# A fifth gate panel inside the attention passes, and one PSUM bank for the later attention outputs

## The chip, the cores and the metric

The kernel runs on one core of a Trainium2 chip. The metric is the device time of one execution in microseconds. Before the change it is 1691.17 us, the median of three runs that span 1689.38 to 1691.74 us.

## What is computed

Four transformer-like layers run on one sequence of 256 tokens with 1024 channels, all in float32. The first two layers (the "first block") are the ones touched here. Cut to what matters, each of them is

```
h = rms_norm(x, attn_pre_gain);  u = h @ w_in            # q, k, v of two attentions, g_nsa, g_a, g_b
o_a = swa_sink_attention(qa, ka, va, sinks)               # windowed softmax attention with sinks
o_b = g0 * o_compressed + g1 * o_selected + g2 * o_window # gates = sigmoid(g_nsa)
mixed = sigmoid(g_a) * (o_a @ w_branch_a) + sigmoid(g_b) * (o_b @ w_branch_b)
x = x + rms_norm(mixed @ w_out, attn_post_gain)
x = x + rms_norm(conv_ffn(rms_norm(x, ffn_pre_gain), ...), ffn_post_gain)
```

g_a and g_b are 2048 of the columns of `h @ w_in`. The last two layers (the "second block") are feed-forward parts and another attention; the change does not touch them.

## The kernel before, in words

**Precision and tiles.** Every large product is made from split operands: a float32 value is a high part that TensorE takes exactly plus the rest. Activations stand as high and low parts side by side (hsA, hsB: 256 + 256 columns of tokens). A weight chunk of 1 MB lands in one of three raw buffers (`RAW`), ScalarE copies it to the high part (L616), VectorE subtracts to get the low part (L1001, `split_to`), and both stand in one of four slots (`RING`). A *wide* tile takes two matmuls for each of its k steps: the high weights against 512 columns (L1582) and the low weights against 256 (L1587); ScalarE then copies the second half of the bank to `low` (`low_copy`) and VectorE adds the two (`tile_sum`, L1009). A *narrow* tile (`NARROW`) adds three matmuls of 256 columns in place (L1580, L1581, L1586) and needs only one copy by ScalarE (`whole_copy`). Tiles have fixed PSUM banks (`tile_bank`: tile number modulo 4, unless in `EXTRA` or `PLACED`).

**The gate panels.** g_a and g_b are made in eight panels of two tiles each (one tile for a, one for b). The first four (`EARLY`) are narrow tiles, made before and in the first passes of the attention. The other four are wide tiles in the *branch* stage behind the attention, in the order of the list `BRANCH`: products with w_branch ("mix", four tiles of four k steps) alternate with gate panels ("gate", two tiles of eight k steps). Panel j's results go to `gate_place(j)`; ScalarE applies the sigmoid, and GpSimd (POOL) multiplies and adds (L1501 to L1505) into MX; ScalarE and VectorE split that into MS, which the following product with w_out reads (L1698 to L1700). VectorE overwrites TA and SG buffers only once POOL is through with them (`mix_ready`).

**The attention passes.** `MAPS` lists 18 score maps: six of the first attention, then for each of six units one compressed-plus-selected map (br 1) and one window map (br 2). The loop over i is written out on every engine as a software pipeline: in pass i TensorE makes the scores of map i (L1850, L1853), transposes the probabilities of map i - 4 (L1873) and makes the value products of map i - 5 (L1900, L1904). VectorE masks and takes maxima (L1254), ScalarE exponentiates (L619), VectorE inverts the sums (L1280), POOL scales (L1493), ScalarE copies the transposed probabilities out of PSUM (PT, L616). The value products accumulate into output number o: 0 to 5 for the first attention, 6 to 11 for the second, where the products of br 1 open and those of br 2 close the accumulation. Output o sits in bank 2 + o % 2. It leaves PSUM in two steps, a ScalarE copy to hsB (L616) and a VectorE subtraction (L1266, counts `o_done`); TensorE waits for the output before the last one that used the bank. Gate panel 3 is made in passes 1 and 3 (`early_tile`), and the first two tiles of mix 0 in passes 21 and 22.

**Queues.** SP issues all weight loads in chunk order; a load waits until VectorE has split the chunk three places earlier. In the attention the splits reach two chunks past panel 3, that is mix 0 and gate panel 4; the split of the next chunk (mix 1) stands at the end of the passes.

## Time and profile before

| quantity | value |
|---|---|
| median of 3 runs | 1691.17 us (1689.38 to 1691.74) |
| profiled execution, first to last instruction (span) | 1688.0 us |
| PE busy / weight loads busy | 1672.5 us (99%) / 1443.9 us (86%) |
| DVE / ACT / POOL busy | 1215.7 / 1034.5 / 698.7 us |
| DMA, mean rate | 182 GB/s |
| chain that ended last | PE 92%, DVE 3%, ACT 2%, DMA 2% |
| granted TensorE clock | 1.000 over the span |

The profile gives the profiled execution's span; no time of its own around the span is shown for it. The span is 3.2 us under the median of the runs (1.4 to 3.7 us under the three of them), which is the start and end that the span leaves out. Matmuls are pipelined and their ends are modelled, so the start of one row to the start of the next is the reading to trust, not the duration in the row. First-block layer 1 has its attention passes from about 84 to 132 us and its branch stage to about 171 us; layer 2 repeats them some 367 us later.

### The profile page before, as it was taken

What the parts mean: (1) busy time and instruction counts of PE and PEld (TensorE: products, weight loads), DVE (VectorE), ACT (ScalarE), POOL (GpSimd) and SP (SyncE); (2) the same over time, 40 slices, a digit from 0 to 9 for tenths busy, and PEclk for the clock granted to TensorE, in tenths of its full rate; (3) what the DMA queues carried; (4) which work ended last, traced back from release to release, by engine and by line L of the source; (5) the groups of instructions that cost most, each with busy time, mean ns of one, the idle gap of its engine ahead of it and who ended that gap; (6) DMA issues with size and microseconds to landing.
All of it is one profiled execution on the core that took longest, in us unless ns stands there. A gap on an engine that the chain in (4) does not pass through costs nothing.

```text
span 1688.0 us, 26353 instructions
## 1 busy us (share of the span) xinstructions
PE 1672.5 (99%) x9878; PEld 1443.9 (86%) x9878; DVE 1215.7 (72%) x1810; ACT 1034.5 (61%) x1901; POOL 698.7 (41%) x662
## 2 busy tenths in 40 slices
PE   8999999999999999999999999999999999999998
PEld 7968888889968988888888979888898889788887
DVE  7877799958868899867664757666576647576663
ACT  6787766656786766565554657554655536575543
POOL 4154176601255276407750052663076600527630
PEclk9999999999999999999999999999999999999999
DMA  8925586565816666649666626866496565358662
GB/s 242 245 69 175 144 231 178 178 218 164 238 27 200 180 195 174 233 128 256 184 199 200 225 75 181 219 173 226 126 250 190 185 224 201 99 150 215 184 212 75
DMA packets 416354, 306.67 MB, mean 182 GB/s; under 512 B 10179, under 2 KB 369013, under 8 KB 416226
## 3 DMA queue, kind: packets, MB, share of 16 engines
q1 hardware_dynamic: 415536, 304.44, 61.6%
q8 instruction: 79, 1.29, 0.3%
q0 software_dynamic: 688, 0.53, 0.1%
q14 instruction: 49, 0.40, 0.1%
q10 hardware_dynamic: 2, 0.00, 0.0%
HBM read 303.89 MB, written 1.05 MB: 181 GB/s over the span
## 4 chain that ended last, share of the span: by engine, by line
PE 92%; DVE 3%; ACT 2%; DMA 2%; issue 1%; SPq 0%; DVEq 0%; ACTq 0%
PE bank L1582 31%; PE bank L1587 15%; PE bank L1698 9%; PE bank L1700 9%; PE bank L1699 9%; PE bank L1661 3%; PE bank L1658 3%; PE bank L1650 3%; DMA raw<-in_w_in 1%; PE bank L1580 1%; DVE whl L1001 1%; PE bank L1581 1%; PE bank L1586 1%; PE bank L1631 1%; PE bank L1904 1%; PE bank L1873 1%
## 5 line engine op out<-in xcount | busy, mean ns | idle before, releaser
L1001 DVE TENSOR_TENSOR whl<-raw,whl 128x1024 fp32r<-128x1024 f32 (+2 forms) x572 | 741.4, 1319 | 174.1 <-ACT whl L616 169.5
L616 ACT ACTIVATE whl<-raw 128x1024 fp32r<-128x1024 f32 (+2 forms) x572 | 581.5, 1040 | 162.1 <-PE bank L1700 102.0
L1582 PE MATMUL bank<-hsA,whl 128*128 128x512 f32 x2112 | 668.5, 396 | 0.0
L1587 PEld LDWEIGHTS bank<-hsA,whl 128*128 128x128 f32 x2112 | 396.8, 188 | 92.5
L1587 PE MATMUL bank<-hsA,whl 128*128 128x256 f32 x2112 | 415.2, 278 | 0.0
L1582 PEld LDWEIGHTS bank<-hsA,whl 128*128 128x128 f32 x2112 | 324.3, 189 | 2.6 <-issue 2.2
L616 ACT ACTIVATE low<-bank 128x256 f32<-128x256 f32 (+1 forms) x356 | 133.4, 379 | 256.3 <-PE bank L1582 237.0
L1442 POOL TENSOR_TENSOR HB<-CB,UB 128x256 f32<-128x256 f32 x88 | 123.7, 1406 | 337.8 <-ACT CB L619 337.2
L1698 PE MATMUL bank<-whl,hid 128*128 128x512 f32 x528 | 205.9, 390 | 0.0
L1700 PE MATMUL bank<-whl,hid 128*128 128x512 f32 x528 | 205.4, 389 | 0.0
L1699 PE MATMUL bank<-whl,hid 128*128 128x512 f32 x528 | 205.4, 389 | 0.0
L1009 DVE TENSOR_TENSOR UB<-bank,low 128x256 f32<-128x256 f32 x264 | 109.0, 417 | 111.2 <-ACT low L616 111.1
L1443 POOL TENSOR_TENSOR hid<-CB,UB 128x256 fp32r<-128x256 f32 x88 | 145.0, 1648 | 0.0
L1442 POOL TENSOR_TENSOR HB<-CB 128x256 f32<-128x256 f32 x44 | 63.1, 1434 | 139.0 <-ACT CB L619 139.0
L1700 PEld LDWEIGHTS bank<-whl,hid 128*128 128x128 f32 x528 | 99.1, 188 | 20.7
L1699 PEld LDWEIGHTS bank<-whl,hid 128*128 128x128 f32 x528 | 99.1, 188 | 20.4
L1698 PEld LDWEIGHTS bank<-whl,hid 128*128 128x128 f32 x528 | 99.1, 188 | 20.1
L1338 DVE SCALAR_TENSOR_TENSOR CB<-UB,convT,CB 128x256 f32<-128x256 f32 x176 | 114.0, 706 | 0.0
L1444 POOL TENSOR_TENSOR hid<-HB,hid 128x256 fp32r<-128x256 f32 x132 | 109.6, 830 | 10.3
L1661 PE MATMUL bank<-hsA,whl 128*128 128x256 f32 x448 | 92.6, 284 | 0.3 <-DVE whl L1001 0.3
L1658 PE MATMUL bank<-hsA,whl 128*128 128x256 f32 x448 | 90.5, 283 | 0.0
L1520 POOL MEMSET CU<- 128x4 f32 x2 | 0.2, 103 | 191.0 <-DVE U L1009 191.0
(234 smaller groups left out, 2355.5 us busy)
## 6 DMA issues: line engine op xcount, KB each, us to landing
raw<-in_ffn_w_up SPq DMA_DIRECT2D x176, 512.0 KB, 5.3
raw<-in_ffn_w_down SPq DMA_DIRECT2D x120, 512.0 KB, 4.5
raw<-in_w_in SPq DMA_DIRECT2D x96, 512.0 KB, 6.5
raw<-in_ffn_w_gate SPq DMA_DIRECT2D x88, 512.0 KB, 4.0
raw<-in_w_out SPq DMA_DIRECT2D x32, 512.0 KB, 4.6
raw<-in_ffn_w_down SPq DMA_DIRECT2D x24, 256.0 KB, 3.0
G<-in_norm_g SPq DMA_DIRECT2D x12, 512.0 KB, 7.5
raw<-in_cmp_w SPq DMA_DIRECT2D x8, 512.0 KB, 6.4
```

Source lines behind the costliest of these rows:

```text
L616: return nc.scalar.activation(out_, in_, func, **kw)
L1001: v.tensor_tensor(lo, w_, hi, ALU.subtract).then_inc(wlo_ready, 1)
L1338: ins = v.scalar_tensor_tensor(y[:, n, :], UB[:, j % 2, n, k:S + k], convT[:, k, at:at + 1], y[:, n, :], ALU.mult, ALU.add)
L1442: g_.tensor_tensor(HB[:, j % 2, :], x, y, ALU.mult)
L1443: seq.link(g_.tensor_tensor(dst[:, 0:S], x, y, ALU.mult))
L1582: return mm(out_[:, 0:2 * n], whi[slot][:, at:at + P], rhs[:, 0:2 * n], start=x == 0, stop=False, **g32)
L1587: return mm(out_[:, n:2 * n], wlo[slot][:, at:at + P], rhs[:, 0:n], start=False, stop=False, **g32)
L1658: return mm(out_, whi[c % RING][:, at(m, k):at(m, k) + P], both(k, 1), start=False, stop=j == 0 and k == KD - 1, **g32)
L1661: return mm(tile_bank(t + m)[:, S:2 * S], wlo[c % RING][:, at(m, k):at(m, k) + P], hsA[:, k, 0:S], start=False, stop=j > 0 and k == KD - 1 ...
L1698: mm(y, hi, whi[s][:, x * HALF:x * HALF + HALF], start=k == k_first, stop=False, **g32)
L1699: mm(y, lo, whi[s][:, x * HALF:x * HALF + HALF], start=False, stop=False, **g32)
L1700: ins = mm(y, hi, wlo[s][:, x * HALF:x * HALF + HALF], start=False, stop=k == k_end, **g32)
```

## The change

`EARLY` becomes 5. Gate panel 4 becomes two narrow tiles in bank 3, each cut into four quarters of two k steps (six matmuls of 256 columns). Quarters are made in passes 12 to 15 (first tile) and 17 to 20 (second tile), between the transposes and the value products. Since bank 3 holds the tiles, outputs 6 to 11 all use bank 2, and TensorE waits before opening output o (o > 6) for the output just before it. ScalarE copies the finished tiles in passes 16 and 21 into a new buffer SG4. Panel 4's chunk comes ahead of mix 0's; one more chunk (gate panel 5) is split in passes 18 to 20. The branch stage keeps three gate panels, with panel 7 between mix 2 and mix 3 in place of panels 6 and 7.

```diff
@@ -79,8 +79,8 @@
 
 
 
-EARLY = 4
-BRANCH = [("mix", 0), ("gate", 4), ("mix", 1), ("gate", 5), ("mix", 2), ("gate", 6), ("gate", 7), ("mix", 3)]
+EARLY = 5
+BRANCH = [("mix", 0), ("gate", 5), ("mix", 1), ("gate", 6), ("mix", 2), ("gate", 7), ("mix", 3)]
 SKEW = 4
 RINGP = 5
 
@@ -243,6 +243,7 @@
     st = sb("st", [P, RINGP, 4, 4])[0]
     stc = sb("stc", [P, 4, 16])[0]
     KC = sb("KC", [P, 2, 2 * N_CMP])[0]
+    SG4 = sb("SG4", [P, 2, S])[0]
     VC = sb("VC", [P, 8, HD], at=cq_at)[0]
 
 
@@ -407,6 +408,7 @@
     EXTRA = {t + m: 4 + m for t in EXTRA for m in range(2)}
 
     PLACED = {p["early"][3][1] + m: 2 + m for p in PLAN.one for m in range(2)}
+    PLACED.update({p["early"][4][1] + m: 3 for p in PLAN.one for m in range(2)})
     PLACED.update({p["fill"] + m: 4 + m for p in PLAN.one for m in range(2)})
 
     NARROW = {t + m for L, p in enumerate(PLAN.one) for _, t in p["in"][3 if L else 1:6] + p["early"] for m in range(2)} | \
@@ -428,13 +430,19 @@
 
         if j == 3:
             return tm[:, :, :]
+        if j == 4:
+            return SG4[:, :, :]
         return SGE[:, 2 * j:2 * j + 2, :] if j < EARLY else SG[:, 2 * (j % 2):2 * (j % 2) + 2, :]
+
+    def o_bank(o):
+
+        return bank[2 + o % 2 if o < 6 else 2]
 
     def o_places(o):
 
         g, qb, hs = UNITS[o % 6]
         j0, nj = 4 * (o // 6) + hs[0] // 2, len(hs) // 2
-        src = bank[2 + o % 2][:, 0:nj * P].rearrange("d (j q) -> d j q", q=P)
+        src = o_bank(o)[:, 0:nj * P].rearrange("d (j q) -> d j q", q=P)
         return (lambda part: hsB[:, j0:j0 + nj, part * S + qb * P:part * S + qb * P + P]), src
 
     def score_place(i, x, keys):
@@ -791,7 +799,7 @@
                         f(HCV[:, :, 0:N_CMP].rearrange("p (g r) c -> p g r c", g=2),
                           x.rearrange("p (g c) -> p g c", g=2).unsqueeze(2).broadcast_to([P, 2, 4, N_CMP]),
                           ACT.Gelu_apprx_tanh, bias=b1).then_inc(cmp_hid, 1)
-            third, fourth = p["early"][2][1], p["early"][3][1]
+            third, fourth, fifth = [p["early"][j][1] for j in (2, 3, 4)]
             whole_copy(third, gate_place(2)[:, 0, :])
             act.preload_act_table_set("natural_log_exp_and_others")
             whole_copy(third + 1, gate_place(2)[:, 1, :])
@@ -813,10 +821,12 @@
                     act.wait_ge(pv_done, done + m + 1)
                     dst, src = o_places(o)
                     f(dst(0), src, ACT.Copy).then_inc(o_hi, 1)
+                if i in (16, 21):
+                    whole_copy(fifth + i // 21, gate_place(4)[:, i // 21, :])
                 m = i - SKEW
                 if m == len(MAPS) + 1:
                     low_copy(p["fill"] + 1)
-                    split_to(p["early"][3][0] + 3)
+                    split_to(p["early"][4][0] + 3)
                 if 0 <= m < len(MAPS):
                     act.wait_ge(pt_ready, done + m + 1)
                     if m >= 2:
@@ -846,8 +856,10 @@
                 if i == 2:
                     act.wait_ge(cmp_x, L + 1)
                     f(PC[:, :, :, 0:N_CMP], PC[:, :, :, 0:N_CMP], ACT.Exp, scale=SCALE).then_inc(cmp_e, 1)
+                if i in (18, 19):
+                    split_to(p["early"][4][0] + 2, i - 18)
                 if m == len(MAPS) - 1:
-                    split_to(p["early"][3][0] + 3, 0)
+                    split_to(p["early"][4][0] + 3, 0)
 
 
             def sigmoids(j):
@@ -858,7 +870,7 @@
                 if 0 < j < 3:
                     low_copy(p["fill"] + 1 + j)
                 if j == 0:
-                    act.wait_ge(tile_out, fourth + 2)
+                    act.wait_ge(tile_out, fifth + 2)
                 sigmoids(j)
 
             def mixed_hi(x):
@@ -880,7 +892,7 @@
                 if kind == "gate":
                     act.wait_ge(tile_out, t + 2)
                     sigmoids(x)
-                if kind == "gate" and x == 6:
+                if kind == "gate" and x == 7:
                     mixed_hi(2)
             mixed_hi(3)
             nxt = token_major(n0 + 1, p["up"][0][1])
@@ -1280,6 +1292,8 @@
                     v.reciprocal(s_[:, 3, 0:nh], s_[:, 1, 0:nh]).then_inc(inv_ready, 1)
                 if i < 2:
                     split_to(p["early"][3][0] + 2, i)
+                if i in (19, 20):
+                    split_to(p["early"][4][0] + 2, i - 19)
                 if i == 2:
                     cmp_scores()
                 if i == 4:
@@ -1315,7 +1329,7 @@
                             split_to(c + 3 if x else c + 2)
                     if x == 0:
                         split_to(c + 3)
-                if kind == "gate" and x == 6:
+                if kind == "gate" and x == 7:
                     mixed_lo(2)
             mixed_lo(3)
             nxt = token_major(n0 + 1)
@@ -1765,6 +1779,22 @@
                 c, t = p["early"][j]
                 chunk_here(c)
                 tile(t + m, c, [(in_pair(m, k), hsA[:, k, :]) for k in range(KD)], beside)
+
+            def gate_quarter(m, quarter):
+
+                c, t = p["early"][4]
+                out_ = tile_bank(t + m)[:, 0:S]
+                if quarter == 0:
+                    chunk_here(c)
+                    pe.wait_ge(o_done, 12 * L + 6)
+                    pe.wait_ge(tile_out, t + m)
+                for k in range(2 * quarter, 2 * quarter + 2):
+                    hi, lo = [w_[c % RING][:, in_pair(m, k):in_pair(m, k) + P] for w_ in (whi, wlo)]
+                    mm(out_, hi, hsA[:, k, 0:S], start=k == 0, stop=False, **g32)
+                    mm(out_, hi, hsA[:, k, S:2 * S], start=False, stop=False, **g32)
+                    ins = mm(out_, lo, hsA[:, k, 0:S], start=False, stop=k == KD - 1, **g32)
+                if quarter == 3:
+                    ins.then_inc(sum_ready, 1)
 
             first = 3 if THREE[n0] else 1
             for c in range(10):
@@ -1879,6 +1909,8 @@
                     for qb in range(2):
                         ins = nc.tensor.transpose(bank[1][:, S + qb * P:S + qb * P + P], PC[:, qb, :, :].rearrange("p h c -> p (h c)"), ident)
                     ins.then_inc(cmp_t, 1)
+                if 12 <= i < 21 and i != 16:
+                    gate_quarter(i // 17, i - (17 if i > 16 else 12))
                 m = i - SKEW - 1
                 if 0 <= m < len(MAPS):
                     u, br = MAPS[m]
@@ -1890,18 +1922,18 @@
                     if m < 2:
                         pe.wait_ge(tile_out, fourth + 2)
                     if br < 2 and o >= 2:
-                        pe.wait_ge(o_done, 12 * L + o - 1)
+                        pe.wait_ge(o_done, 12 * L + (o if o > 6 else o - 1))
 
                     def every_other(ap, e):
                         return ap.rearrange("k (j e q) -> k j e q", e=2, q=P)[:, :, e, :]
                     if br == 1:
                         for x, h in enumerate(hs):
                             j, r = x // 2 * P, HD * (x % 2)
-                            mm(bank[2 + o % 2][r:r + HD, j:j + P], VC[:, h, :], PCT[:, qb * P:qb * P + P],
+                            mm(o_bank(o)[r:r + HD, j:j + P], VC[:, h, :], PCT[:, qb * P:qb * P + P],
                                start=j == 0, stop=False, **g32)
                     for kb in range(qb + 1):
                         for e in range(2):
-                            ins = mm(bank[2 + o % 2][HD * e:HD * e + HD, 0:n // 2], V1[:, br, kb, HD * g:HD * g + HD],
+                            ins = mm(o_bank(o)[HD * e:HD * e + HD, 0:n // 2], V1[:, br, kb, HD * g:HD * g + HD],
                                      every_other(PT[:, m % 2, kb * n:kb * n + n], e),
                                      start=br == 0 and kb == 0, stop=br != 1 and kb == qb, **g32)
                     ins.then_inc(pv_done, 1)
```

## Rows read from the trace of the kernel before

**Rows 1.** The page's part 1: busy time of each engine.

```profile
PE 1672.5 (99%) x9878; PEld 1443.9 (86%) x9878; DVE 1215.7 (72%) x1810; ACT 1034.5 (61%) x1901; POOL 698.7 (41%) x662
```

**Rows 2.** Waits of PE, whole span (us in total, times, longest).

```profile
PE bank L1904 <- ACT PT L616: 1.9, 6, 0.4
```

**Rows 3.** Stretches (us, engines busy, PEclk, DMA share, GB/s): passes 12 on; branch stage.

```profile
109.50:125.80 16.30, 16.30 (x151) 10.31 (x149) 10.40 (x56) 14.78 (x46) 10.53 (x21) 1.00 0.01 2
...
132.20:150.00 17.80, 17.80 (x104) 15.49 (x103) 14.84 (x19) 14.42 (x31) 10.66 (x10) 1.00 0.71 184
```

**Rows 4.** Timeline of PE, passes 13 to 21 in extract (start, us, instruction); layer 2.

```profile
112.38 0.44 PE L1900 MATMUL bank<-U,VC 128*64 128x128 f32 x4
...
116.82 0.69 PE L1853 MATMUL bank<-KSW,QR 64*128 64x512 f32 x1
...
117.88 0.66 PE L1873 MATMUL bank<-const,PB 128*128 128x128 f32 x4
118.47 0.66 PE L1904 MATMUL bank<-PT,V 128*64 128x128 f32 x8
119.06 0.66 PE L1873 MATMUL bank<-const,PB 128*128 128x128 f32 x4
...
124.99 0.44 PE L1900 MATMUL bank<-U,VC 128*64 128x128 f32 x4
...
480.63 0.69 PE L1853 MATMUL bank<-KSW,QR 64*128 64x512 f32 x1
...
484.26 0.69 PE L1853 MATMUL bank<-KSW,QR 64*128 64x512 f32 x1
```

**Rows 5.** Timeline of PE: branch stage, first tile of gate panel 4 and first of mix 1.

```profile
132.28 0.39 PE L1582 MATMUL bank<-hsA,whl 128*128 128x512 f32 x1
...
137.85 0.39 PE L1582 MATMUL bank<-hsB,whl 128*128 128x512 f32 x1
```

**Rows 6.** Timeline of PE: a whole narrow tile in pass 1, first and last rows.

```profile
84.68 0.38 PE L1580 MATMUL bank<-hsA,whl 128*128 128x256 f32 x1
84.90 0.28 PE L1581 MATMUL bank<-hsA,whl 128*128 128x256 f32 x1
...
87.53 0.28 PE L1581 MATMUL bank<-hsA,whl 128*128 128x256 f32 x1
87.73 0.48 PE L1850 MATMUL bank<-U 64*128 64x256 f32 x1
```

**Rows 7.** Timeline of PE: two 256-column matmuls between transposes, entry of the feed-forward part.

```profile
199.58 0.66 PE L1631 MATMUL bank<-const,H 128*128 128x128 f32 x4
199.99 0.48 PE L1650 MATMUL bank<-hsA,whl 128*128 128x256 f32 x2
200.31 0.60 PE L1631 MATMUL bank<-const,H 128*128 128x128 f32 x4
```

**Rows 8.** Timeline of DVE: subtractions of outputs 6, 8 and 10.

```profile
113.38 0.42 DVE L1266 TENSOR_TENSOR hsB<-bank,hsB 128x256 fp32r<-128x256 f32 x1 [0.54 <-ACT hsB L616]
...
120.34 0.29 DVE L1266 TENSOR_TENSOR hsB<-bank,hsB 128x128 fp32r<-128x128 f32 x1 [0.45 <-ACT hsB L616]
...
124.82 0.29 DVE L1266 TENSOR_TENSOR hsB<-bank,hsB 128x128 fp32r<-128x128 f32 x1 [1.83 <-ACT hsB L616]
```

**Rows 9.** Timeline of POOL: sum of panel 5; first rows of panels 6 and 7.

```profile
161.28 1.63 POOL L1505 TENSOR_TENSOR MX<-TA 128x256 f32<-128x256 f32 x1
169.72 0.75 POOL L1501 TENSOR_TENSOR TA<-TA,SG 128x256 f32<-128x256 f32 x1 [6.80 <-DVE TA L1009]
...
174.07 0.74 POOL L1501 TENSOR_TENSOR TA<-TA,SG 128x256 f32<-128x256 f32 x1 [0.24 <-DVE TA L1009]
```

**Rows 10.** Timeline of DVE: low part of panel 7's mixture.

```profile
176.99 0.42 DVE L1296 TENSOR_TENSOR MS<-MX,MS 128x256 fp32r<-128x256 f32 x1 [1.90 <-ACT MS L616]
```

**Rows 11.** Timeline of PE: first and ninth matmul of the product with w_out.

```profile
171.29 0.39 PE L1698 MATMUL bank<-whl,MS 128*128 128x512 f32 x1
...
173.11 0.39 PE L1700 MATMUL bank<-whl,MS 128*128 128x512 f32 x1
```

## The prediction, made before the change was run

> **What bounds the kernel now.** I read the page's busy times first. They say PE 99% [rows 1], but a busy PE row is a pipelined row, so that alone proves nothing. The waits of PE come next: in the attention it waited for the copy of transposed probabilities, 1.9 us in six waits over both layers [rows 2], and the timeline has those in passes 5 to 9, ahead of the first quarter. Then the stretches: from pass 12 to pass 20 PE has no idle time, while ACT is busy 14.8 of 16.3 us and DVE 10.4; in the branch stage PE has none either [rows 3]. What decides is the distance from one start to the next in PE's timeline. Transposes start at 117.88, value products at 118.47, the next transposes at 119.06 [rows 4]: 0.59 us each, again and again, and layer 2 keeps the same step of 3.63 us for two passes [rows 4]. Other engines' waits would make such distances uneven. So PE's own stream sets the time from pass 10 of the attention to the end of the branch stage, with ACT close behind.
>
> The consequence for this change: quarters placed in passes 12 to 20 find no holes. They push the passes apart by what they cost, and the time comes back in the branch stage as one gate panel less. The forecast is a difference of two nearly equal terms.
>
> **Part 1, what leaves the branch stage.** Gate panel 4 begins at 132.28 and the next chunk at 137.85 [rows 5]: 5.57 us of PE in each layer, with nothing else limiting it. Wide or narrow makes no difference in columns: 8 x (512 + 256) against 8 x 3 x 256.
>
> **Part 2, what the quarters cost.** Inside a narrow tile 22 matmuls pass between 84.90 and 87.53, 0.12 us each, so six of them are 0.72. The whole tile takes 87.73 - 84.68 = 3.05 us where 24 x 0.12 = 2.88, so going from attention products into it and out again costs 0.17 [rows 6]. If every quarter pays that on top of what was there, it costs 0.89: the upper bound. But the 0.59 us from four transposes to the value products is partly the start-up of a waited group. Where no wait follows, four transposes take 199.99 - 199.58 = 0.41, and two matmuls of 256 columns behind them, with a waited group after, 0.32 [rows 7]. Six would take 0.32 + 4 x 0.12 = 0.80, so from transposes to value products through a quarter would be 1.21 instead of 0.59: 0.62 more. That is the lower bound, and the nearest row for a quarter without waits of its own. The first quarter of each tile has waits (for the chunk, for bank 3, for the tile before), so I give it the 0.89. Per layer: 6 x 0.62 + 2 x 0.89 = 5.5 us, between 8 x 0.62 = 5.0 and 8 x 0.89 = 7.1. Parts 1 and 2 together: -0.07 us per layer, between -0.6 and +1.55.
>
> **Part 3, one bank for outputs 6 to 11.** Now TensorE may open output o only when the one before has been copied by ACT and subtracted by DVE. Both stand in queues: ACT's copy behind the exponentials of the pass before, DVE's subtraction behind the maxima. There are five such hand-overs per layer, in passes 13, 15, 17, 19 and 21. Pass 13: the subtraction of output 6 ended at 113.38 + 0.42 = 113.80, and the value products would start at 112.38 + 0.89 + 0.62 = 113.89 with two quarters ahead [rows 4, 8]: no stall. Pass 17, with no quarter in pass 16 to lend time: products wanted at 119.06 + 0.59 + 0.89 = 120.54 in the old frame, subtraction over at 120.34 + 0.29 = 120.63 [rows 4, 8], some 0.2 late with the signal. Pass 21 has no quarter: wanted at 124.99, subtraction over at 124.82 + 0.29 = 125.11 [rows 4, 8], again 0.2. Passes 15 and 19 have slack: a quarter each, and no exponentials any more in passes 18 and 19. So 0.4 us per layer. Below: 0, if ACT, which gets more room as passes grow, is earlier. Above: each hand-over as late as output 6's in the old frame, 113.80 - 112.38 = 1.4 behind the wanted time, less the 0.62 of a quarter: 0.8 at four places and 1.4 at pass 21, 4.6 us per layer.
>
> The Trainium skill, in "Perfetto Trace Analysis", section "Matmuls", says that independent matmul groups should rotate through PSUM banks so that the emptying of one lies beside the next. It speaks against this part. By the rule every hand-over would be exposed, and the sum would be near the upper end just given; by the rows the quarter itself lies beside the emptying. No row of before has all outputs in one bank.
>
> **Part 4, the shorter branch stage.** Taking a panel from between mix 2 and mix 3 leaves POOL, DVE and ACT less time for the last mixtures. In the old frame mix 2's matmuls end at 132.28 + 4 x 5.57 = 154.56, the sum of panel 5 on POOL at 161.28 + 1.63 = 162.91 [rows 5, 9]. DVE may write panel 7's sums only then, into the buffer of panel 5. PE needs the first of those sums at mix 3's third tile, 154.56 + 1.5 x 5.57 = 162.9: a stall of up to 0.5, or none, since POOL's 1.63 lies beside a DVE split that now comes later. From there to the last low part: DVE's sums, a half split, low parts, sums of mix 3, an estimated 3.4 us of DVE work; panel 6 on POOL, 174.07 - 169.72 less 0.24 of waiting = 4.1 [rows 9]; a signal, 0.2; panel 7 to the end of its low part, 176.99 + 0.42 - 174.07 = 3.3 [rows 9, 10]. Together 11.0, so 173.1 to 173.9. PE reads that part after 33 matmuls of the product with w_out, (173.11 - 171.29) / 8 = 0.2275 us each, so at 171.29 + 7.5 - 5.57 = 173.2 [rows 11]; before, it wanted it at 178.8 and had it at 177.4. The old slack of 1.4 us is gone. I take 0.3 us per layer, between 0 and 1.3.
>
> **Edits costed at nothing.** The chunk split moved into passes 18 to 20 (two ScalarE copies, two VectorE subtractions) falls where both have idle time: no exponentials after pass 17, and DVE sat idle 1.83 us before output 10's subtraction [rows 8]. SP loads one chunk earlier, into a stretch with a DMA share of 0.01 [rows 3]. The two narrow copies replace two `low` copies on ACT, and two sums of DVE go. The fifth sigmoid pair moves ahead of panel 5's copies. If ACT's cover were gone, these would feed the hand-overs of part 3.
>
> **The sum.** Per layer -0.07 + 0.4 + 0.3 = +0.63, for two layers +1.3 us. The profiled span goes from 1688.0 to 1689.3. The runs' median stands 3.2 us above the span, so 1692.5 us. A measurement of this kernel can tell about 0.2% (3.4 us) from no change; this forecast is no difference to be seen. Its own range, with parts 2 to 4 within half of their bounds, is 1689.5 to 1694.5. Chance 0.66.
>
> **Rivals.**
>
> *The passes have hidden holes (faster).* Weight loads are busy 10.3 of 16.3 us in the later passes against 15.5 of 17.8 in the branch stage [rows 3]. If the difference were room, eight quarters would cost nothing: -2 x 5.57 + 1.4 for parts 3 and 4 = -9.7, 1681.4 us. For it: that share, and passes that are as long as ACT's work. Against: the even starts [rows 4]; short matmuls (64 x 512, 128 x 128) need few weight loads for their time. Chance 0.08. The skill's "Perfetto Trace Analysis", section "Identifying the Most-Contended Engine", calls matmul busy time a poor measure and wants the share of weight loads instead; by that reading the attention has headroom and this rival is the forecast. The distances between starts agree with the first half of the rule and not with the second.
>
> *A quarter saves nothing (slower).* Each costs 0.89 us [rows 6]: +1.55 per layer, with parts 3 and 4 +2.25, for both +4.5, 1695.7 us. For it: the only whole narrow tile inside attention passes shows that price. It decides from about 0.82 us per quarter on. Chance 0.16.
>
> *The single bank is late at every hand-over (slower).* The place is TensorE's wait for `o_done` before products of br 1 in passes 13 to 21; the price is 4.6 us per layer, so 2 x (-0.07 + 4.6 + 0.3) = +9.7, 1700.9 us. It decides once the subtraction ends more than 1.2 us (transposes and quarter) after the closing products. For it: ACT is busy 91% of that stretch [rows 3], and its copy queues behind exponentials. Against: slower passes give ACT room, and half the hand-overs were costed with none needed. Chance 0.10, mostly in a milder form near 1697.
>
> **How the numbers follow.** Likeliest case: 1692.5. Faster by over 0.2%: the first rival, 0.08. Slower by over 0.2%: 0.16 + 0.10 = 0.26. Within: 0.66. The range is 1688.5 (lower bounds of all parts, -1.2 us, with the runs' own scatter) to 1698.0, which takes in the second rival and the mild form of the third; outside stay the first rival and the far end of the third.
>
> **What would show it.** Right: two value-product starts around a quarter 1.2 us apart; passes 12 to 20 longer by 5 to 6 us per layer; branch stage shorter by 5.6; new waits of PE L1900 on DVE L1266 of a few tenths, in passes 17 and 21; at most a few tenths at L1698 or L1700 on MS. Wrong: passes no longer than before (first rival), quarters 0.9 us apart in price (second), waits on L1266 above 1 us (third), or PE waits at the end of the branch stage of over 1 us, which would be part 4 mis-sized.

## The result and the profile after

| | kernel before | changed kernel |
|---|---|---|
| median of 11 runs each | 1690.89 us | 1694.30 us |
| lowest to highest | 1688.76 to 1691.74 | 1693.18 to 1695.51 |
| profiled execution (span) | 1691.17 (1688.0) | 1694.68 (1692.9) |
| ratio, 95% interval | | 1.0023 [1.0015, 1.0031] |

The change costs 3.4 us by the medians (3.9 by the ratio). The prediction said 1692.5 with a range of 1688.5 to 1698.0, which holds the result. The likeliest case was "no difference to be seen", below 0.2%, with a chance of 0.66; the result lies just above that bound, in the case that had 0.26. It is on the side that the sum of +1.3 us pointed to, but at two to three times its size. So most of what follows asks where the other two microseconds come from.

The page's first part, after, answers [rows 1]:

```profile
PE 1675.2 (99%) x9910; PEld 1447.0 (85%) x9910; DVE 1213.2 (72%) x1806; ACT 1032.7 (61%) x1901; POOL 694.5 (41%) x662
```

PE has 32 more matmuls: wide tiles of 512 and 256 columns have become narrow ones of three times 256, with equal columns. The page's sums tell nothing more. The waits of PE over the whole span (us in total, times, longest) say where to look:

```profile
PE bank L1936 <- ACT PT L624: 2.0, 6, 0.4
PE bank L1932 <- DVE hsB L1278: 1.1, 4, 0.4
...
PE bank L1596 <- DVE SG L1021: 0.3, 2, 0.2
```

The first answers [rows 2] and is unchanged. The other two are new: L1932 is the first value product of a hand-over of the single bank, L1596 a tile of the branch stage.

**The layer in pieces.** Between the transposes of pass 12 and the transposes behind the product with w_out, nothing comes in from outside the change, so I take the distance between their starts as the measure S of every kernel below. PE's timeline before, at both ends:

```profile
110.63 0.66 PE L1873 MATMUL bank<-const,PB 128*128 128x128 f32 x4
...
191.70 1.03 PE L1631 MATMUL bank<-const,H 128*128 128x128 f32 x8
```

Before, S was 191.70 - 110.63 = 81.07 us, in layer 2 the same to 0.01. PE's timeline after (start, us, instruction):

```profile
111.45 0.66 PE L1903 MATMUL bank<-const,PB 128*128 128x128 f32 x4
111.86 0.36 PE L1793 MATMUL bank<-hsA,whl 128*128 128x256 f32 x1
...
112.75 0.65 PE L1936 MATMUL bank<-PT,V 128*64 128x256 f32 x4
113.33 0.66 PE L1903 MATMUL bank<-const,PB 128*128 128x128 f32 x4
...
114.78 0.44 PE L1932 MATMUL bank<-U,VC 128*64 128x128 f32 x4
...
122.28 0.66 PE L1936 MATMUL bank<-PT,V 128*64 128x128 f32 x8
122.87 0.66 PE L1903 MATMUL bank<-const,PB 128*128 128x128 f32 x4
124.60 0.66 PE L1932 MATMUL bank<-U,VC 128*64 128x128 f32 x8 [0.36 <-DVE hsB L1278]
...
131.49 0.66 PE L1903 MATMUL bank<-const,PB 128*128 128x128 f32 x4
132.35 0.44 PE L1932 MATMUL bank<-U,VC 128*64 128x128 f32 x4 [0.21 <-DVE hsB L1278]
...
139.64 0.39 PE L1596 MATMUL bank<-hsA,whl 128*128 128x512 f32 x1
...
145.21 0.39 PE L1596 MATMUL bank<-hsB,whl 128*128 128x512 f32 x1
...
148.32 0.47 PE L1596 MATMUL bank<-hsB,whl 128*128 128x512 f32 x1 [0.16 <-DVE SG L1021]
...
151.26 0.47 PE L1596 MATMUL bank<-hsA,whl 128*128 128x512 f32 x1
...
156.92 0.39 PE L1596 MATMUL bank<-hsB,whl 128*128 128x512 f32 x1
...
173.65 0.39 PE L1712 MATMUL bank<-whl,MS 128*128 128x512 f32 x1
...
194.35 1.04 PE L1645 MATMUL bank<-const,H 128*128 128x128 f32 x8
```

S is now 194.35 - 111.45 = 82.90 us: +1.83 per layer, and layer 2 gives the same +1.83. To read it: the distance from a pass's four transposes to its value products was 0.59 us in all of passes 12 to 21 [rows 4]. In pass 12 it is now 112.75 - 111.45 = 1.30. Passes 14, 15, 18 and 20 also show 1.30 and pass 19 shows 1.29, so a quarter costs 0.71, in layer 2 too (within 0.01). Pass 16, which has none, still shows 0.59. Three passes show more: 13 has 1.45, which is 0.15 above 1.30; 17 has 124.60 - 122.87 = 1.73, 0.43 above; 21, which has no quarter, has 0.86, 0.27 above 0.59.

| per layer, us | forecast | measured |
|---|---|---|
| panel 4 leaves the branch stage | -5.57 | -5.57 |
| eight quarters | +5.5 | 8 x 0.71 = +5.68 |
| hand-overs of the bank | +0.4 (0, 0.2, 0.2) | +0.85 (0.15, 0.43, 0.27 in passes 13, 17, 21) |
| mix 1 and gate panel 6 | 0 | +0.57 |
| product with w_out | +0.3 | +0.29 |
| sum | +0.63 | +1.82 |

The fourth line was not forecast. Mix 1 begins at 145.21 and panel 6 at 151.26, which is 6.05 us instead of 5.57; panel 6 takes 156.92 - 151.26 = 5.66, 0.09 more than 5.57. For the last line, 194.35 - 173.65 = 20.70 stands against 20.41 before.

Two layers give +3.66 of the 4.9 us between the spans. A further 0.84 us arises at the start, ahead of anything changed. The transposes of HE early in the attention start at 80.75 after (L1775) and at 79.91 before (L1761). None of the nine experiments touches this part, and in their profiles the same instruction starts anywhere from 79.35 to 81.91, so I put the 0.84 down to scatter of that size; its cause is not shown. About 0.4 us lies in the last feed-forward part and was not followed up. It does not recur between the medians, whose difference of 3.4 is accounted for by 3.66.

### The profile page after: what moved, and what is told of

It reads as the page before. It is cut to its first block, busy times and chain, and to the rows that moved or that the text cites. A ratio compares the mean times of both kernels' runs of the same rounds, so it can differ in the third digit from the quotient of the medians.

```text
span 1692.9 us, 26417 instructions
## 1 busy us (share of the span) xinstructions
PE 1675.2 (99%) x9910; PEld 1447.0 (85%) x9910; DVE 1213.2 (72%) x1806; ACT 1032.7 (61%) x1901; POOL 694.5 (41%) x662
## 3 DMA queue, kind: packets, MB, share of 16 engines
q8 instruction: 79, 1.29, 0.3%
## 4 chain that ended last, share of the span: by engine, by line
PE 88%; ACT 4%; DVE 3%; DMA 2%; issue 1%; POOL 1%; SPq 1%; DVEq 0%; ACTq 0%; POOLq 0%
PE bank L1596 30%; PE bank L1601 15%; PE bank L1712 9%; PE bank L1714 8%; PE bank L1713 8%; PE bank L1675 3%; PE bank L1672 3%; PE bank L1664 2%; DMA raw<-in_w_in 2%; DVE whl L1013 1%; ACT whl L624 1%; PE bank L1594 1%; PE bank L1645 1%; PE bank L1936 1%; PE bank L1595 1%
## 5 line engine op out<-in xcount | busy, mean ns | idle before, releaser
L1596 PE MATMUL bank<-hsA,whl 128*128 128x512 f32 x2080 | 658.5, 396 | 0.0
L1601 PEld LDWEIGHTS bank<-hsA,whl 128*128 128x128 f32 x2080 | 390.8, 188 | 91.0
L1601 PE MATMUL bank<-hsA,whl 128*128 128x256 f32 x2080 | 408.9, 278 | 0.0
L1596 PEld LDWEIGHTS bank<-hsA,whl 128*128 128x128 f32 x2080 | 319.4, 189 | 2.9 <-issue 2.6
L624 ACT ACTIVATE low<-bank 128x256 f32<-128x256 f32 x352 | 131.4, 379 | 258.6 <-PE bank L1596 239.2
L1712 PE MATMUL bank<-whl,hid 128*128 128x512 f32 x528 | 205.9, 390 | 0.0
L1714 PE MATMUL bank<-whl,hid 128*128 128x512 f32 x528 | 205.5, 389 | 0.0
L1714 PEld LDWEIGHTS bank<-whl,hid 128*128 128x128 f32 x528 | 99.1, 188 | 20.6
L1712 PEld LDWEIGHTS bank<-whl,hid 128*128 128x128 f32 x528 | 99.1, 188 | 20.1
L1675 PE MATMUL bank<-hsA,whl 128*128 128x256 f32 x448 | 92.6, 284 | 0.0
L1672 PE MATMUL bank<-hsA,whl 128*128 128x256 f32 x448 | 90.5, 283 | 0.0
```

The source lines that it names most:

```text
L624: return nc.scalar.activation(out_, in_, func, **kw)
L1596: return mm(out_[:, 0:2 * n], whi[slot][:, at:at + P], rhs[:, 0:2 * n], start=x == 0, stop=False, **g32)
L1601: return mm(out_[:, n:2 * n], wlo[slot][:, at:at + P], rhs[:, 0:n], start=False, stop=False, **g32)
L1672: return mm(out_, whi[c % RING][:, at(m, k):at(m, k) + P], both(k, 1), start=False, stop=j == 0 and k == KD - 1, **g32)
L1675: return mm(tile_bank(t + m)[:, S:2 * S], wlo[c % RING][:, at(m, k):at(m, k) + P], hsA[:, k, 0:S], start=False, stop=j > 0 and k == KD - 1 ...
L1712: mm(y, hi, whi[s][:, x * HALF:x * HALF + HALF], start=k == k_first, stop=False, **g32)
```

## The experiments

S of each kernel (layer 1; layer 2 agrees within 0.05), against 81.07 before and 82.90 of the changed kernel, with the run time and, where there are several runs, the ratio to the kernel before:

| kernel | S | per layer | median | ratio |
|---|---|---|---|---|
| bank only | 85.80 | +4.7 | 1700.21 | 1.0052 [1.0037, 1.0068] |
| sigmoids of panel 4 later | 82.16 | +1.1 | 1693.53 | 1.0014 [1.0005, 1.0023] |
| quarters in odd passes | 82.87 | +1.8 | 1694.61 | 1.0025 [1.0015, 1.0034] |
| three edits together | 81.99 | +0.92 | 1692.97 | 1.0006 [0.9997, 1.0015] |
| half splits one pass later | 81.77 | +0.70 | 1692.57 | 1.0007 [0.9998, 1.0016] |
| one half split on ACT | 81.34 | +0.28 | 1690.94 | 1.0003 [0.9993, 1.0012] |
| whole tiles | 85.47 | +4.4 | 1699.62, one run | |
| quarters behind the value products | 85.76 | +4.7 | 1701.32, one run | |
| own place for panel 7 | 82.58 | +1.5 | 1694.80, one run | |

The kernel before was timed again beside them: 1691.19 us beside the first four rows, 1690.32 beside "one half split on ACT", 1691.24 beside the rest. So a median is to be held against its own partner. The last three ratios include 1: what separates those kernels from each other is S, which repeats to 0.05 us, and not the run time.

### The single bank alone

The kernel before, with the new bank rule and nothing else:

```diff
+    def o_bank(o):
+        return bank[2 + o % 2 if o < 6 else 2]
...
-                        pe.wait_ge(o_done, 12 * L + o - 1)
+                        pe.wait_ge(o_done, 12 * L + (o if o > 6 else o - 1))
```

> The kernel before with one edit: outputs 6 to 11 use bank 2 and TensorE waits for the output just before. No quarters, four early panels. Theory A (a quarter lies beside the emptying of the bank and hides most of it; alone, the single bank is dear): in the kernel before, the value products of passes 13, 15 and 17 start at 112.38, 116.01 and 119.64, and the subtractions they would now wait for end at 113.80, 117.39 and 120.63, so they come 1.0 to 1.5 us late; with stalls that give ACT room in between, 2.5 to 4.5 us per layer over the five hand-overs, 1696 to 1700 us in all. Rival B (the hand-over costs little whatever lies beside it, and what the changed kernel lost comes from the cut of the tile): under 0.5 us per layer, 1691 to 1692 us. The branch stage keeps its length, 4 chunks of 5.57 us from gate panel 4 on, in both.

S is 85.80: 4.7 us per layer, above what was expected. PE's waits and its timeline in passes 13 and 17:

```profile
PE bank L1904 <- ACT PT L620: 5.3, 4, 1.5
PE bank L1904 <- DVE hsB L1270: 3.5, 6, 1.1
```

```profile
113.02 0.66 PE L1877 MATMUL bank<-const,PB 128*128 128x128 f32 x4
...
115.17 0.44 PE L1904 MATMUL bank<-U,VC 128*64 128x128 f32 x4 [1.49 <-ACT PT L620]
...
123.05 0.66 PE L1877 MATMUL bank<-const,PB 128*128 128x128 f32 x4
...
124.78 0.66 PE L1904 MATMUL bank<-U,VC 128*64 128x128 f32 x8 [1.07 <-DVE hsB L1270]
```

From transposes to value products it takes 2.15, 1.80, 1.73, 1.10 and 0.86 us in passes 13, 15, 17, 19 and 21, where 0.59 was enough: 1.56 + 1.21 + 1.14 + 0.51 + 0.27 = 4.69. This is the whole of the 4.7. All five hand-overs are late, not only two.

The profile names ACT's copy to PT for the waits of passes 13 and 15. By the code that is not what these products wait for: the copy to PT that pass 13 needs is the one of pass 12, and it was over by 113.14. They wait for the subtraction of output 6, which ends at 115.02, and the product starts 0.15 later at 115.17; the profile names the instruction that ended last, here the copy for the next pass, 0.03 later. All of these are waits for the bank.

 With the quarters in, the five cost 0.15, 0, 0.43, 0 and 0.27. So the quarters hide 3.8 of 4.7 us. In pass 17 the sum is exact: 1.14 - 0.71 = 0.43. In pass 21, which has no quarter, the 0.27 is the same in both kernels.

The Trainium skill ("Perfetto Trace Analysis", section "Matmuls") says that independent groups should rotate through PSUM banks. Alone, the single bank costs what the rule warns of, and this run agrees with it; the changed kernel keeps to one bank and pays 0.85, since other matmuls fill the time in which the bank is emptied.

### The sigmoids of panel 4 behind mix 0

```diff
-                sigmoids(j)
+                if j < 4:
+                    sigmoids(j)
...
+                    if n_ == 1:
+                        sigmoids(4)
```

The second place is in ACT's loop over `BRANCH`, behind the copies of gate panel 5 and the chunk splits around them.

> The changed kernel with the fifth panel's two sigmoids moved on ACT from before gate panel 5's chunk splits to behind them. In the trace of the changed kernel the third tile of mix 1 starts 0.33 us late behind the sum of panel 5, mix 1 takes 6.05 us in place of 5.57 and the gate panel after it 5.66. Theory A (these 0.61 us of sigmoids on ACT delay the split, the split delays VectorE's sums of panel 5, and these hold TensorE): mix 1 back to 5.57 to 5.65, the next panel to 5.57, 0.5 to 0.6 us per layer, 1693.1 to 1693.4 us in all against 1694.3. Rival B (VectorE and POOL contend for SBUF there, whatever ACT does): mix 1 stays at 6.0, 1694.3 us.

S falls by 0.74, to 82.16. PE's timeline shows mix 1 at its old length:

```profile
145.49 0.39 PE L1599 MATMUL bank<-hsB,whl 128*128 128x512 f32 x1
...
151.06 0.39 PE L1599 MATMUL bank<-hsA,whl 128*128 128x512 f32 x1
```

151.06 - 145.49 = 5.57; panel 6 takes 5.58. Together that is the 0.57. A further 0.17 is gained in the product with w_out (20.53 instead of 20.70 in layer 1; in layer 2 it is 20.59, a gain of 0.12). This settles the unforecast line. The chain in the changed kernel is one of queues. ACT, then DVE:

```profile
142.71 0.72 ACT L627 ACTIVATE SG<-SG 128x256 f32<-128x256 f32 x2
143.32 2.00 ACT L624 ACTIVATE whl<-raw 128x1024 fp32r<-128x1024 f32 x2
```

```profile
144.41 3.43 DVE L1013 TENSOR_TENSOR whl<-raw,whl 128x1024 fp32r<-128x1024 f32 x2 [2.37 <-ACT whl L624]
147.77 0.74 DVE L1021 TENSOR_TENSOR SG<-bank,low 128x256 f32<-128x256 f32 x2
```

The fifth sigmoid pair takes 143.32 - 142.71 = 0.61 us on ACT, ahead of the high parts of a chunk. DVE waits for these (2.37 idle), subtracts for 3.4 us, and only then forms the sums of gate panel 5, which free the two banks that mix 1 needs for its third tile. That tile would have started at 145.21 + 5.57 / 2 = 147.99 and started at 148.32. DVE's busy share of 72% hides this. What counts is that the bank of a matmul stands behind a 3.4 us job in a queue whose start is set by another queue.

### Quarters in the odd passes

The hand-overs fall in odd passes. So two quarters each went into passes 13, 15 and 17, one each into 19 and 21:

```diff
-                if 12 <= i < 21 and i != 16:
-                    gate_quarter(i // 17, i - (17 if i > 16 else 12))
+                for tile_, quarter_ in {13: [(0, 0), (0, 1)], 15: [(0, 2), (0, 3)], 17: [(1, 0), (1, 1)], 19: [(1, 2)], 21: [(1, 3)]}.get(i, []):
+                    gate_quarter(tile_, quarter_)
```

The second tile's copy moves from pass 21 to 22 with it.

> The changed kernel with the same eight quarters in other passes: two in pass 13, two in 15, two in 17, one in 19, one in 21, none in 12, 14, 18 and 20; the second copy moves from pass 22 of ACT in place of 21. All hand-overs of bank 2 that TensorE waits for then have one or two quarters in front. In the changed kernel passes 13, 17 and 21 lose 0.15, 0.43 and 0.27 us to the hand-over, 0.85 per layer. Theory A (the hand-overs make that loss): the idle time in front of L1932 goes to 0 to 0.2 us in all, each quarter still costs 0.70 to 0.73 us, 0.7 to 0.85 us per layer gained, about 1692.7 us. Rival B (the loss belongs to the number of switches between transposes, quarter and value products): eight switches become five, which would save 3 x 0.17 = 0.5 us per layer in the cost of the quarters, with the idle time left as it is. Rival C (two quarters in one pass delay the transposed probabilities for ACT and the next scores): other waits of 0.3 us and more appear in passes 14, 16 and 18, nothing gained.

S stays (82.87): nothing is gained. Rival C expected that, but not in this way: passes 14, 16 and 18 keep their 0.59 and show no new wait. Passes 15 and 17 show 2.02 = 0.59 + 2 x 0.71 + 0.01, and pass 21 shows 1.30, so the waits of 17 and 21 are gone; pass 13 keeps its 0.14. But pass 19 has 1.94 for one quarter:

```profile
127.02 0.65 PE L1903 MATMUL bank<-const,PB 128*128 128x128 f32 x4
...
128.96 0.44 PE L1932 MATMUL bank<-U,VC 128*64 128x128 f32 x4 [0.58 <-ACT PT L624]
```

The time removed at two places (0.43 + 0.27) came back at a third (0.64). The profile names ACT's copy to PT again, but again that is the copy for the next pass; the one that pass 19 needs, in the first row below, was long over. ACT's timeline, then DVE's:

```profile
126.54 0.60 ACT L624 ACTIVATE PT<-bank 128x512 f32<-128x512 f32 x1 [1.01 <-PE bank L1903]
127.03 1.05 ACT L624 ACTIVATE whl<-raw 128x1024 fp32r<-128x1024 f32 x1
127.98 0.37 ACT L624 ACTIVATE hsB<-bank 128x256 fp32r<-128x256 f32 x1
```

```profile
128.39 0.42 DVE L1278 TENSOR_TENSOR hsB<-bank,hsB 128x256 fp32r<-128x256 f32 x1 [2.31 <-ACT hsB L624]
```

The half split that the change moved into pass 18 holds ACT for 1 us. The copy of output 9 stands behind it, and the subtraction behind that. The subtraction ends at 128.81, and the product starts 0.15 later, at 128.96: this is still a wait for the bank. From the transposes of pass 18 to that start the chain takes 128.96 - 125.85 = 3.11 us. PE needs 0.59 + 0.58 + 1.30 = 2.47 for the same way with one quarter in it, so it waits 0.64. In the changed kernel two quarters lie on the way, one of them in pass 18, and PE needs 128.79 - 125.62 = 3.17, just longer than the chain; there the same split cost nothing.

### Three edits together

Quarters in the odd passes, the later sigmoids, and a place of its own for gate panel 7:

```diff
+        if j == 7:
+            return SGE[:, 0:2, :]
...
-                    if x >= EARLY + 2:
-                        dve.wait_ge(mix_ready, 8 * L + x - 1)
```

> The two edits above together, and panel 7 written to the place of panel 0 in place of that of panel 5, so that VectorE's sums of panel 7 don't wait for POOL. Theory A: what is left of the change is 8 x 0.71 - 5.57 = +0.11 us per layer; 1691.2 us, no difference to the kernel before (1690.9), with the passes 5.7 us longer per layer and the branch stage 5.6 us shorter. The late start of the last k step of the product with w_out (0.29 us per layer) goes too, because the sums of panel 7 come some 2 us earlier. Rival B (something of the change costs apart from the three waits, 1.8 us per layer in all): 1692.5 us or more stay.

S is 81.99, +0.92 per layer, where the remaining wait of pass 19 (0.64) and that of pass 13 (0.14) with 0.11 from the quarters make 0.89. All chunks of the branch stage take 5.57 and the product with w_out 20.41, as before the change. So the branch terms are gone, as expected; that nearly the whole gain should come was not met, since the attention's term is moved rather than removed. The median of 1692.97 lies where Rival B had it, but what stays is again waits for the bank, not another cost of the change.

### The half splits one pass later

ACT's half splits go from passes 18 and 19 to 19 and 20, DVE's from 19 and 20 to 20 and 21, all else as in the three edits:

```diff
-                if i in (18, 19):
-                    split_to(p["early"][4][0] + 2, i - 18)
+                if i in (19, 20):
+                    split_to(p["early"][4][0] + 2, i - 19)
```

> three_fixes with the two halves of the chunk split moved by one pass: on ACT from passes 18 and 19 to 19 and 20, on DVE from 19 and 20 to 20 and 21. In three_fixes the value products of pass 19 came 1.94 us behind their transposes where 1.30 is the price of a quarter, with 0.58 us idle behind ACT's copy of the transposed probabilities. Theory A (the ACT half split of 1.05 us in pass 18, which has no quarter there, holds that copy up): pass 19 takes 1.30 to 1.40, pass 20 at most 0.2 more than before; the stretch from the transposes of pass 12 to those behind the product with w_out goes from 81.99 to 81.4 to 81.6 us in both layers (81.07 in the kernel before), about 1692.0 us where three_fixes had 1692.97. Rival B (ACT's copies of outputs hold it up): pass 19 stays at 1.94.

S is 81.77, a little more than expected. Pass 19 is back at 1.30, so the half split was the cause; what it had held up there was the copy of output 9, not the copy to PT that Theory A names. But pass 21 shows 1.70. ACT in pass 20, and PE's waits for a bank over both layers:

```profile
131.27 1.05 ACT L626 ACTIVATE whl<-raw 128x1024 fp32r<-128x1024 f32 x1
132.22 0.27 ACT L626 ACTIVATE hsB<-bank 128x128 fp32r<-128x128 f32 x1
```

```profile
PE bank L1935 <- DVE hsB L1283: 0.7, 2, 0.3
```

The second half now stands ahead of the copy of output 10. The same microsecond of ACT reappears as a wait in whichever hand-over follows it, unless a quarter covers it.

### One half split on ACT in the passes

So only the first half stays in a pass (19); the second falls to the split that ACT does anyway at the end of the attention. DVE takes its halves in passes 20 and 22.

```diff
-                if i in (18, 19):
-                    split_to(p["early"][4][0] + 2, i - 18)
+                if i == 19:
+                    split_to(p["early"][4][0] + 2, 0)
```

> later_splits with the second ACT half of the chunk split moved from pass 20 to behind the last copy of transposed probabilities in pass 21, and VectorE's from 21 to 22. In later_splits pass 21 took 1.70 us from transposes to value products where a quarter makes it 1.30, because ACT's copy of output 10 stood behind that half split (131.27 to 132.3). Theory A (every loss of the change is a place in ACT's queue, and all are now named): pass 21 at 1.30, the stretch from the transposes of pass 12 to those behind the product with w_out 81.35 us in both layers, that is 0.28 us above the kernel before: 0.11 for 8 quarters at 0.71 against one wide panel at 5.57, and 0.14 in pass 13. In all about 1691.8 us, no difference. Rival B (the split has to be paid somewhere in the passes or at their end, since ACT has no idle time left): pass 21 at 1.30 but the same 0.4 us appears in pass 22 or at the first tiles behind the passes, stretch 81.7.

PE's timeline in pass 21:

```profile
129.76 0.66 PE L1906 MATMUL bank<-const,PB 128*128 128x128 f32 x4
...
131.06 0.44 PE L1935 MATMUL bank<-U,VC 128*64 128x128 f32 x4
```

There is no wait, 131.06 - 129.76 = 1.30, and pass 19 has the same distance. S is 81.34, +0.28 per layer: 0.11 by which eight quarters cost more than the panel they replace, and 0.15 in pass 13. The ratio is 1.0003 [0.9993, 1.0012]. It is the best version that I ran, and it does not beat the kernel before: with all waits but the one of pass 13 gone, the change is worth nothing. Whether that last 0.15 can be removed was not tried; without it the change would still cost 0.1 us per layer.

### Whole tiles instead of quarters

Is it the cutting into quarters that costs? All four quarters of a tile in one pass, 12 and 17:

```diff
+                for tile_, quarter_ in {12: [(0, 0), (0, 1), (0, 2), (0, 3)], 17: [(1, 0), (1, 1), (1, 2), (1, 3)]}.get(i, []):
+                    gate_quarter(tile_, quarter_)
```

> The changed kernel with the same matmuls uncut: all four quarters of the first tile in pass 12, of the second in pass 17. Theory A (a quarter costs its six matmuls and nothing for the cut, since the start-up of the waited group behind it is hidden): transposes to value products 0.59 + 4 x 0.72 = 3.45 us, in both passes, the same sum as 8 quarters at 0.71; but the hand-overs without a quarter grow, 0.3 to 0.5 in pass 13, about 1.2 in pass 15, 0.5 in 19, 0.27 in 21, so the stretch from the transposes of pass 12 to those behind the product with w_out comes to 84 to 84.5 us (82.90 in the changed kernel). Rival B (every cut costs 0.17 us, so six fewer cuts save 1.0 us per layer, and hand-overs depend little on where the quarters are): 82.0 us.

PE's timeline in passes 12 and 13:

```profile
111.19 0.66 PE L1903 MATMUL bank<-const,PB 128*128 128x128 f32 x4
...
114.64 0.65 PE L1936 MATMUL bank<-PT,V 128*64 128x256 f32 x4
115.23 0.66 PE L1903 MATMUL bank<-const,PB 128*128 128x128 f32 x4
...
116.33 0.44 PE L1932 MATMUL bank<-U,VC 128*64 128x128 f32 x4 [0.45 <-DVE hsB L1278]
```

114.64 - 111.19 = 3.45, or 2.86 for 24 matmuls: 0.715 per six, the same as a quarter. The cuts cost nothing. What is lost is cover: passes 13, 15, 19 and 21 exceed the 0.59 us by 0.51, 1.21, 1.36 and 0.28, and S ends at +4.4, 1 us above the expectation, in which the stall of pass 19 was taken at 0.5.

### Quarters behind the value products

The same quarters, placed after each pass's value products instead of between transposes and value products (the block moves behind the increment of `pv_done`).

> The changed kernel with each quarter made behind the value products of its pass in place of ahead of them. Theory A (only the order on TensorE between closing and opening an output counts, and a quarter lies between them either way): passes 12 to 21 take the same time within 0.4 us per layer, stretch 82.5 to 83.3 us (82.90). Rival B (the place between transposes and value products is worth its cover of ACT's copy of the transposed probabilities): transposes to value products grow past 0.59 us in several passes, 1 us per layer and more is lost. Rival C (behind the value products a quarter pays both switches, 0.17 us): 8 x 0.17 = 1.4 us per layer, 84.3.

PE's timeline, passes 12 and 13:

```profile
112.92 0.65 PE L1934 MATMUL bank<-PT,V 128*64 128x256 f32 x4
113.51 0.39 PE L1793 MATMUL bank<-hsA,whl 128*128 128x256 f32 x1
...
114.33 0.60 PE L1903 MATMUL bank<-const,PB 128*128 128x128 f32 x4
...
115.67 0.44 PE L1930 MATMUL bank<-U,VC 128*64 128x128 f32 x4 [0.74 <-ACT PT L624]
```

From value products to the next transposes it takes 114.33 - 112.92 = 1.41, where 0.58 was enough, so here a quarter costs 0.83. And the wait in pass 13 is back (115.67 - 114.33 = 1.34 instead of 0.59), with 0.99, 1.73 and 1.13 in passes 15, 17 and 19. The first theory is wrong here, and what its two rivals name is there at once: the price is 0.12 higher (8 x 0.12 = 0.96) and the waits grow from 0.85 to 2.83. Together that is 2.9, and 82.90 + 2.9 = 85.8 is what S shows.

The cover that is lost is not quite the one that Rival B names, since here too the products of pass 13 start 0.15 behind the end of a subtraction (115.51). The distances from the transposes of pass 12 to the value products of pass 13 tell more: 3.32 in the kernel with the single bank alone, 3.33 in the changed kernel, 3.32 with the quarters in odd passes, 3.33 here. From the transposes of pass 16 to the value products of pass 17 it is 2.90, 2.91 and 2.90 in the single-bank kernel, the changed one and this one. So with exponentials in the pass the emptying does not start from the closing products: it runs from the transposes before them, through ACT's copy to PT and its exponentials to the output's copy and DVE's subtraction, and takes the same time wherever the quarters stand. A quarter covers it if it lies between those transposes and the reopening. Two do so in pass 12 and 13 of the changed kernel (0.15 of waiting), one here (0.75), none in the single-bank kernel (1.56).

### A place of its own for panel 7, alone

The diff of the three edits, alone, on the changed kernel.

> The changed kernel with panel 7 written to the place of panel 0 in place of that of panel 5, and without VectorE's wait for POOL before it. The product with w_out takes 20.70 us to the transposes behind it in the changed kernel and 20.41 before. Theory A (the sums of panel 7 wait for POOL's work on panel 5 and everything for the last mixture is late behind them): 20.41 again, the stretch from the transposes of pass 12 at 82.6 us. Rival B (the last mixture is late because mix 1 and the panels before it were late behind the fifth sigmoid): 20.6 to 20.7 stays, as in late_sigmoid it went to 20.53 to 20.59.

```profile
174.72 0.39 PE L1712 MATMUL bank<-whl,MS 128*128 128x512 f32 x1
...
195.13 0.38 PE L1645 MATMUL bank<-const,H 128*128 128x128 f32 x2
```

195.13 - 174.72 = 20.41: the 0.29 is gone, and mix 1 is still long, 6.04. So the tail's term comes from DVE's wait until panel 5's place is free, as part 4 had it. But the later sigmoids alone, with that wait in place, already took 0.17 and 0.12 us of it in the two layers. So in the changed kernel the lateness behind the fifth sigmoid pair fed this wait, and without it 0.12 and 0.18 us would have been left.

## Why the prediction was right, and where it was short

**What bounds the kernel: right.** The passes had no room. Eight quarters made them longer by 5.68 us, and the branch stage became shorter by the 5.57 of [rows 5]. With the hand-overs, passes 12 to 20 grew by 6.27 us per layer (131.49 - 111.45 = 20.04 against 13.77), a little over the 5 to 6 that were to show it. The first rival (hidden holes, 1681.4 us) is refuted, and with it the reading of the Trainium skill's "Perfetto Trace Analysis", section "Identifying the Most-Contended Engine", in which weight loads are the measure, as far as it is read as room for more matmuls. Passes 12 to 22 after (stretch, its length, busy us of PE, PEld, DVE, ACT and POOL, PEclk, DMA share, GB/s):

```profile
111.40:135.30 23.90, 23.26 (x206) 17.28 (x204) 12.18 (x55) 17.42 (x48) 9.76 (x20) 1.00 0.14 45
```

The weight loads went from 63% of the passes [rows 3] to 72%, without reaching the 87% of the branch stage, and yet each quarter was paid in full. One reason that the prediction gave against this rival was wrong: the short matmuls do not need few weight loads. [rows 3] has 149 loads for 151 matmuls there, and 103 for 104 in the branch stage; the loads were only shorter, 10.31 / 149 = 0.07 us against 0.15.

**Part 2, the quarter: right within its bounds.** It costs 0.71, between 0.62 and 0.89. The step that split the quarters in two kinds was wrong: the first quarter of a tile, with its waits, costs 0.71 like the others, not 0.89. That the sum came within 0.2 (5.5 against 5.68) is partly luck: two errors of opposite sign, 0.09 too little for six quarters and 0.18 too much for two. The second rival (0.89 each) is refuted too. The whole narrow tile of [rows 6], from which it took its price, paid for the way in and out of other products; between transposes and value products only 0.71 shows. The lower bound let six matmuls hide the start-up of the group behind them; they do not: 1.30 less the 0.41 of four transposes and the 0.72 of six matmuls leaves 0.17, as 0.59 - 0.41 = 0.18 did without a quarter.

**Part 3, the hand-overs: the step that failed by a factor of two.** Forecast 0, 0.2 and 0.2, measured 0.15, 0.43 and 0.27. When the bank is free in pass 17 was forecast to the hundredth. DVE in pass 17 of the changed kernel, answering [rows 8]:

```profile
124.16 0.29 DVE L1278 TENSOR_TENSOR hsB<-bank,hsB 128x128 fp32r<-128x128 f32 x1 [0.56 <-ACT hsB L624]
```

It ends at 124.45, which is 2.17 after the closing products at 122.28; in the old frame it was 120.63 - 118.47 = 2.16. Two other things were off. The moment from which PE waits was taken with the quarter at 0.89, since it was the first of its tile, so the dear quarter was credited as cover: PE wanted the bank at +1.30 behind the transposes, not at +1.48. And the signal from DVE's end to PE's start takes 124.60 - 124.45 = 0.15, which the text left at "with the signal". In pass 13 that signal alone is the loss: the subtraction ends at 114.63, just when PE wants the bank (113.33 + 1.30), and the products start at 114.78. The upper bound of 4.6 us was close to what the single bank costs by itself (4.7), and the rival built on it, late at every hand-over, is true of that kernel and not of this one: quarters cover it. Its condition (subtraction over 1.2 us behind the closing products) was badly put, for it left out the 0.59 us from those products to the next transposes: in pass 17, 2.17 plus the signal of 0.15 stands against 0.59 + 1.30 = 1.89, and the difference is the 0.43.

**Part 4, the tail: right**, 0.29 against 0.3, with the cause it named; that the size fits so well is luck, since 0.12 to 0.17 of it came through the fifth sigmoid pair, which the forecast did not have. No wait at L1712 to L1714 shows as a group of its own; the loss stands in distances. Part of it shows at the 34th matmul of the product, the first that reads the low part of panel 7, in PE's timeline:

```profile
181.30 0.50 PE L1712 MATMUL bank<-whl,MS 128*128 128x512 f32 x1
```

By 33 x 0.2275 = 7.5 us behind 173.65 it should start at 181.16, so 0.14 is lost up to here; the rest falls later in the same product. Own place for panel 7 removes the whole.

**The edits costed at nothing: the second step that failed.** "The fifth sigmoid pair moves ahead of panel 5's copies" was given no price and no cover was named for it on ACT. It cost 0.57 us per layer (and 0.12 to 0.17 in the tail), 1.1 of the 2.4 us by which the two layers exceed the forecast. Of the same list, the half splits in passes 18 to 20 did cost nothing in this kernel, but not because ACT and DVE had idle time there, as the forecast had it: only because quarters stood beside them. With the quarters elsewhere the same splits cost 0.64. The line "if ACT's cover were gone, these would feed the hand-overs of part 3" was right, and measured.

**The numbers.** Corrected term by term the forecast would have been 2 x 1.82 = +3.6 us, 1694.5 on the median of before; measured 1694.3. That the case with the largest chance (no difference) gave way to +0.23% is the sum of three errors of one sign, per layer 0.57 for the sigmoids and 0.45 for the hand-overs, both from queues on ACT and DVE, and 0.18 for the quarters on PE. Neither of the two rivals that made up the chance of this case is what happened: a quarter costs 0.71 and not 0.89, and the bank is late at three hand-overs by 0.15 to 0.43, not at all of them.

## What to carry to other kernels

If the starts on the bounding engine stand at even distances, as here, look for no room there, whatever the busy shares of other engines say: the work moved in cost its full length, and such a move is worth only what is lost or won at its edges. A bank that is emptied and refilled without a second one is cheap as long as independent work of the same length stands beside the emptying. Find out where the emptying starts: here it was not at the products that close the output but at ACT's work ahead of the output's copy, so work between transposes and value products covered it and work behind the value products did less. When an instruction is moved, write down for each engine's queue what stands behind it and who waits for that: a 0.6 us sigmoid pair ahead of a chunk split reached TensorE through two queues, and a 1 us split ahead of an output's copy reached it through a bank. And check a named wait against the code: the profile names the instruction that ended last, which need not be the one that was waited for.

## What the runs showed of the hardware that was not expected

Six matmuls of 256 columns on 128 rows cost 0.71 us between transposes and waited value products (six times 0.12 us), and 0.83 behind the value products. So the start-up of a waited group, part of the 0.59 us of [rows 4], is not hidden by six matmuls ahead of it, contrary to the lower bound of 0.62. A tile accumulated in one bank in four pieces, with other groups into other banks in between, takes no longer than in one piece (0.71 against 0.715 per six). From the end of a subtraction on DVE to the start of the product that waits for it, 0.15 us pass (114.63 to 114.78 and 124.45 to 124.60 in the changed kernel, 128.81 to 128.96 with the quarters in odd passes).
